# First load of an encoder kernel in single k tiles, with the first weight tile split by VectorE

## The reference

```
layer 0:  h = RMSNorm(x) @ w_in        # 2048 x 8192: q, k, v, gate
          per head (8): a = softmax(q1 k1 + bias) - lam * softmax(q2 k2 + bias);  o = a @ v
          x += (head_norm(o) * silu(gate)) @ w_out
layer 1:  h = RMSNorm(x) @ w_in + b    # 2048 x 6144: a, g, z
          u = depthwise_conv31(a * sigmoid(g)); u = silu(LayerNorm(u)) * silu(z)
          x += u @ w_out + b_out
out = RMSNorm(x)
```

## Time and profile before

| | |
|---|---|
| median of 3 runs | 869.5 us (869.18, 869.5, 871.02) |
| span of the profiled execution | 867.2 us (its own time is not listed apart from the three runs) |
| TensorE busy | 855.9 us, 99% |
| VectorE, ScalarE, POOL busy | 567.5, 446.9, 215.6 us |
| mean granted clock of TensorE | 0.998 |
| HBM read | 160.83 MB |

### The profile page before, as it was taken

One profiled execution on the slowest core, in us unless ns is written; L12 is line 12 of the kernel. 1 busy time (PEld: TensorE's weight loads), 2 busy tenths in 40 slices (PEclk: granted clock), 3 DMA queues, 4 the chain that ended last, 5 costly groups with the idle time before them and its releaser, 6 DMA issues.

```text
span 867.2 us, 13867 instructions
## 1 busy us (share of the span) xinstructions
PE 855.9 (99%) x5732; PEld 782.8 (90%) x5732; DVE 567.5 (65%) x896; ACT 446.9 (52%) x582; POOL 215.6 (25%) x74
## 2 busy tenths in 40 slices
PE   8999999999999999999999999999999999999996
PEld 8998899889998899888888899999999999998885
DVE  6556564584456554585454557999999998566651
ACT  6745443455345543567444454455554555694432
POOL 0000000000000000000000006888888888680000
PEclk9999999999999999999999999999999999999999
DMA  9976565544554565543555654555555556549502
GB/s 338 395 259 234 164 195 193 184 162 157 196 193 145 163 199 190 194 146 116 179 191 194 194 175 164 194 172 175 193 195 171 174 191 196 167 173 340 177 19 97
DMA packets 97856, 163.74 MB, mean 189 GB/s; under 512 B 3296, under 2 KB 38368, under 8 KB 97288
## 3 DMA queue, kind: packets, MB, share of 16 engines
q1 hardware_dynamic: 96320, 160.77, 55.1%
q10 hardware_dynamic: 1480, 2.19, 0.7%
HBM read 160.83 MB, written 3.69 MB: 190 GB/s over the span
## 4 chain that ended last, share of the span: by engine, by line
PE 93%; DMA 3%; DVE 2%; ACT 1%; SPq 0%; issue 0%; ACTq 0%
PE ps_acc L1174 16%; PE ps_acc L1177 16%; PE ps_acc L1176 16%; PE ps_acc L1157 13%; PE ps_acc L1160 13%; PE ps_acc L1159 13%; DMA sb_xs<-in_x 2%; DMA sb_xT<-in_x_turned 1%; PE ps_a L1120 1%; PE ps_d L1120 1%; DVE sb_w_lo L766 1%; PE ps_a L1241 0%; PE ps_a L1240 0%; PE ps_a L1239 0%; PE ps_d L1218 0%; PE ps_d L1217 0%
## 5 line engine op out<-in xcount | busy, mean ns | idle before, releaser
L417 ACT ACTIVATE sb_w_hi<-sb_w_raw 128x2048 fp32r<-128x2048 f32 x141 | 270.1, 1916 | 288.3 <-PE ps_acc L1177 186.4
L766 DVE TENSOR_TENSOR sb_w_lo<-sb_w_raw,sb_w_hi 128x2048 fp32r<-128x2048 f32 x97 | 222.3, 2292 | 170.1 <-ACT sb_w_hi L417 169.9
L1174 PE MATMUL ps_acc<-sb_conv_hi,sb_w_hi 128*128 128x256 f32 x768 | 215.5, 281 | 0.0
L1177 PE MATMUL ps_acc<-sb_conv_hi,sb_w_lo 128*128 128x256 f32 x768 | 214.3, 279 | 0.0
L1176 PE MATMUL ps_acc<-sb_conv_lo,sb_w_hi 128*128 128x256 f32 x768 | 214.2, 279 | 0.0
L408 POOL TENSOR_TENSOR sb_w_lo<-sb_w_raw,sb_w_hi 128x2048 fp32r<-128x2048 f32 x44 | 203.8, 4639 | 41.3 <-ACT sb_w_hi L417 41.3
L961 DVE SCALAR_TENSOR_TENSOR ps_d<-sb_uT,sb_dwT,ps_d 128x256 f32<-128x256 f32 x480 | 188.9, 481 | 4.5 <-ACT ps_d L648 4.5
L1157 PE MATMUL ps_acc<-sb_w_hi,sb_act_hi 128*128 128x512 f32 x384 | 152.4, 397 | 0.0
L1160 PE MATMUL ps_acc<-sb_w_hi,sb_act_lo 128*128 128x512 f32 x384 | 151.5, 394 | 0.0
L1159 PE MATMUL ps_acc<-sb_w_lo,sb_act_hi 128*128 128x512 f32 x384 | 151.5, 394 | 0.0
L1174 PE MATMUL ps_acc<-sb_act_hi,sb_w_hi 128*128 128x256 f32 x512 | 143.7, 281 | 2.0 <-DVE sb_w_lo L802 2.0
(11 more groups left out here) (167 smaller groups left out, 818.2 us busy)
## 6 DMA issues: line engine op xcount, KB each, us to landing
sb_w_raw<-in_attn_w_in SPq DMA_DIRECT2D x61, 1024.0 KB, 5.5
sb_w_raw<-in_conv_w_in SPq DMA_DIRECT2D x64, 512.0 KB, 4.5
sb_w_raw<-in_attn_w_out SPq DMA_DIRECT2D x16, 1024.0 KB, 4.9
sb_w_raw<-in_conv_w_in SPq DMA_DIRECT2D x16, 1024.0 KB, 5.0
sb_w_raw<-in_conv_w_out SPq DMA_DIRECT2D x16, 1024.0 KB, 5.0
sb_w_raw<-in_attn_w_in SPq DMA_DIRECT2D x6, 512.0 KB, 8.1
sb_xT<-in_x_turned SPq DMA_DIRECT2D x4, 512.0 KB, 8.1
sb_xs<-in_x SPq DMA_DIRECT2D x2, 1024.0 KB, 15.7
```

Source lines behind the costliest of these rows:

```text
L417: act.activation(w_hi[slot][:], w_raw[slot][:], ACT.Copy).then_inc(hi_ready, 1)
L766: dve.tensor_tensor(w_lo[slot][:], w_raw[slot][:], w_hi[slot][:].bitcast(F32), ALU.subtract).then_inc(lo_ready, 1)
L1174: pe.matmul(into, left_hi, hi[:, kt], start=(kt == 0 and f % 2 == 0), stop=False, skip_group_check=True)
L1177: ins = pe.matmul(into, left_lo, hi[:, kt], start=False, stop=(kt == KT - 1), skip_group_check=True)
```

## The change

The head is loaded and split in ten pieces (`HEAD`): k tiles 0, 1, 2, 3 singly, and six pairs. SyncE issues per piece the tiles of `xT` and of the weights; the weights of piece 0 are issued by ScalarE behind `vec_all`. VectorE makes the high part of piece 0's weights (`first_hi`), ScalarE that of the others. TensorE runs a single k tile kind by kind: four matmuls high times high, four with `act_lo`, four with `w_lo`, with a wait ahead of each kind; a pair waits once and runs as before. POOL writes `ones` ahead of everything else, TensorE starts on it alone, and runs 9 warm-up matmuls. The warm-up no longer waits for `ident`, nor for `d_free`.

```diff
-HALVED = 3
-WARM_UP = 12
+HEAD = [(k, k + 1) for k in range(CK)] + [(k, k + 2) for k in range(CK, KT, 2)]
+WARM_UP = 9
...
+        def head_piece(p):
+
+            k0, k1 = HEAD[p]
+            return k0 // CK, slice(k0 % CK, (k1 - 1) % CK + 1), k1 % CK == 0
+
+        def pieces_left_open(p):
+
+            return sum(k1 % CK != 0 for _, k1 in HEAD[:p])
+
+        def piece_landed(p):
+
+            slot, _, closes = head_piece(p)
+            return landed[slot] if closes else head_landed[pieces_left_open(p)]
...
-            for q in range(PAIRS):
-                sp.dma_start(xT[:, q * CK:(q + 1) * CK], x_turned[:, q * CK:(q + 1) * CK]).then_inc(x_landed[q], 16)
-                if q < HALVED:
-                    half = q * CK + CK // 2
-                    sp.dma_start(w_raw[q][:, 0:CK // 2], w_in[:, q * CK:half, 0:GW]).then_inc(head_landed[q], 16)
-                    sp.dma_start(w_raw[q][:, CK // 2:], w_in[:, half:(q + 1) * CK, 0:GW]).then_inc(landed[q], 16)
-                else:
-                    load(q, w_in[:, q * CK:(q + 1) * CK, 0:GW])
+            for p, (k0, k1) in enumerate(HEAD):
+                slot, rows, _ = head_piece(p)
+                sp.dma_start(xT[:, k0:k1], x_turned[:, k0:k1]).then_inc(x_landed[p], 16)
+                if p:
+                    sp.dma_start(w_raw[slot][:, rows], w_in[:, k0:k1, 0:GW]).then_inc(piece_landed(p), 16)
             sp.dma_start(table[:], rel_bias).then_inc(table_landed, 16)
...
+            pool.memset(ones[:], 1.0).then_inc(consts_ready, 1)
             pool.memset(grants[:, 0:1], 0.0).then_inc(w_free, RING)
             pool.memset(grants[:, 1:2], 0.0).then_inc(acc_free, 4)
...
             pool.memset(ident[:], 0.0).then_inc(consts_ready, 1)
-            pool.memset(ones[:], 1.0).then_inc(consts_ready, 1)
...
             act.dma_start(vec_all[:], vectors).then_inc(vecs_landed, 16)
-            act.wait_ge(consts_ready, 3)
-
-            act.activation(table_probe, ident[:, 0:1], ACT.Copy)
+            act.dma_start(w_raw[0][:, 0:1], w_in[:, 0:1, 0:GW]).then_inc(piece_landed(0), 16)
+            act.wait_ge(consts_ready, 1)
+
+            act.activation(table_probe, ones[:, 0:1], ACT.Copy)
             act.wait_ge(vecs_landed, 16)
 
-            for q in range(PAIRS):
-                act.wait_ge(x_landed[q], 16)
-                for kt in range(q * CK, (q + 1) * CK):
+            for p, (k0, k1) in enumerate(HEAD):
+                slot, rows, closes = head_piece(p)
+                act.wait_ge(x_landed[p], 16)
+                for kt in range(k0, k1):
                     act.activation(act_hi[:, kt], xT[:, kt], ACT.Copy, scale=vecs[:, G_IN, kt:kt + 1]
                                    ).then_inc(split_hi, 1)
-                if q < HALVED:
-                    act.wait_ge(head_landed[q], 16)
-                    act.wait_ge(w_free, RING)
-                    act.activation(w_hi[q][:, 0:CK // 2], w_raw[q][:, 0:CK // 2], ACT.Copy).then_inc(head_hi, 1)
-                    act.wait_ge(landed[q], 16)
-                    act.activation(w_hi[q][:, CK // 2:], w_raw[q][:, CK // 2:], ACT.Copy).then_inc(hi_ready, 1)
-                else:
-                    high_part(q, q, 1)
+                if p:
+                    act.wait_ge(piece_landed(p), 16)
+                    act.activation(w_hi[slot][:, rows], w_raw[slot][:, rows], ACT.Copy
+                                   ).then_inc(hi_ready if closes else head_hi, 1)
             for i in range(NCH - ST):
...
-            for q in range(PAIRS):
-                dve.wait_ge(x_landed[q], 16)
-                for kt in range(q * CK, (q + 1) * CK):
+            for p, (k0, k1) in enumerate(HEAD):
+                slot, rows, closes = head_piece(p)
+                if p == 0:
+                    dve.wait_ge(piece_landed(0), 16)
+                    dve.tensor_copy(w_hi[slot][:, rows], w_raw[slot][:, rows]).then_inc(first_hi, 1)
+                dve.wait_ge(x_landed[p], 16)
+                for kt in range(k0, k1):
                     dve.wait_ge(split_hi, kt + 1)
                     dve.scalar_tensor_tensor(act_lo[:, kt], xT[:, kt], vecs[:, G_IN, kt:kt + 1],
                                              act_hi[:, kt].bitcast(F32), ALU.mult, ALU.subtract
                                              ).then_inc(x_split, 1)
-                if q < HALVED:
-                    dve.wait_ge(head_hi, q + 1)
-                    dve.tensor_tensor(w_lo[q][:, 0:CK // 2], w_raw[q][:, 0:CK // 2],
-                                      w_hi[q][:, 0:CK // 2].bitcast(F32), ALU.subtract).then_inc(head_lo, 1)
-                    dve.wait_ge(hi_ready, q + 1)
-                    dve.tensor_tensor(w_lo[q][:, CK // 2:], w_raw[q][:, CK // 2:],
-                                      w_hi[q][:, CK // 2:].bitcast(F32), ALU.subtract).then_inc(lo_ready, 1)
+                if p == 0:
+                    dve.wait_ge(first_hi, 1)
+                elif closes:
+                    dve.wait_ge(hi_ready, slot + 1)
                 else:
-                    low_part(q, q)
+                    dve.wait_ge(head_hi, pieces_left_open(p))
+                dve.tensor_tensor(w_lo[slot][:, rows], w_raw[slot][:, rows], w_hi[slot][:, rows].bitcast(F32),
+                                  ALU.subtract).then_inc(lo_ready if closes else head_lo, 1)
             for i in range(NCH - 1):
                 low_part(RING + i, i)
...
-            pe.wait_ge(consts_ready, 3)
...
+            def head_slot(i):
+
+                for p, (k0, k1) in enumerate(HEAD):
+                    slot, rows, closes = head_piece(p)
+                    if slot != i:
+                        continue
+                    if k1 - k0 > 1:
+                        pe.wait_ge(x_split, k1)
+                        pe.wait_ge(lo_ready if closes else head_lo, i + 1 if closes else pieces_left_open(p + 1))
+                        for kt in range(k0, k1):
+                            ins = project_tile(i, 0, act_hi, act_lo, kt)
+                        continue
+                    kt = k0
+                    into = [acc[:, f // 2, (f % 2) * SEQ:(f % 2 + 1) * SEQ] for f in range(GW // P)]
+                    left = [[part[i][:, kt % CK, f * P:(f + 1) * P] for f in range(GW // P)] for part in (w_hi, w_lo)]
+                    pe.wait_ge(split_hi, kt + 1)
+                    if p == 0:
+                        pe.wait_ge(first_hi, 1)
+                    elif closes:
+                        pe.wait_ge(hi_ready, i + 1)
+                    else:
+                        pe.wait_ge(head_hi, pieces_left_open(p))
+                    for f in range(GW // P):
+                        pe.matmul(into[f], left[0][f], act_hi[:, kt], start=(kt == 0 and f % 2 == 0), stop=False,
+                                  skip_group_check=True)
+                    pe.wait_ge(x_split, kt + 1)
+                    for f in range(GW // P):
+                        pe.matmul(into[f], left[0][f], act_lo[:, kt], start=False, stop=False, skip_group_check=True)
+                    pe.wait_ge(lo_ready if closes else head_lo, i + 1 if closes else pieces_left_open(p + 1))
+                    for f in range(GW // P):
+                        ins = pe.matmul(into[f], left[1][f], act_hi[:, kt], start=False, stop=False,
+                                        skip_group_check=True)
+                ins.then_inc(w_free, 1)
 
             def pair_slot(j, i):
                 t, A = i // NCH, A_START + A_PER_PAIR * j
-                head = type(j) is int and j == 0 and i < HALVED
-                if head:
-                    pe.wait_ge(head_lo, i + 1)
-                    pe.wait_ge(x_split, CK * i + CK // 2)
+                if i % NCH == 0:
+                    pe.wait_ge(acc_free, 2 * (4 * j + t + 1))
+                if type(j) is int and j == 0 and i < NCH:
+                    head_slot(i)
                 else:
                     pe.wait_ge(lo_ready, 16 * j + i + 1)
-                if i % NCH == 0:
-                    pe.wait_ge(acc_free, 2 * (4 * j + t + 1))
-                halfway = (lambda: second_half(i)) if head else None
-                if t < 2:
-                    project_turned(i % NCH, t % 2, act_hi, act_lo, halfway)
-                else:
-                    project(i % NCH, t % 2, act_hi, act_lo, halfway)
+                    if t < 2:
+                        project_turned(i % NCH, t % 2, act_hi, act_lo)
+                    else:
+                        project(i % NCH, t % 2, act_hi, act_lo)
...
-            pe.wait_ge(d_free, 2)
+            pe.wait_ge(consts_ready, 1)
             for _ in range(WARM_UP):
                 pe.matmul(bank_d[0][:, 0:P], ones[:], ones[:], start=True, stop=True)
             for i in range(16):
-                if HALVED <= i < PAIRS:
-                    pe.wait_ge(x_split, CK * (i + 1))
                 pair_slot(0, i)
                 if i == 2:
...
```

(27 more changed lines are left out.)

12 lines of the change are left out of this document (6 added, 6 removed).

## The result

The changed kernel takes **871.78 us** (median of 13 runs, 869.59 to 873.51) where the kernel before took 869.54 on the same chip (13 runs, 868.82 to 871.02). The ratio is 1.0025, with a 95% interval of 1.0017 to 1.0033: slower by 2.2 us, a quarter of a per cent. The forecast was no change at 869.5.

The account below looks back on a forecast made before the run. TensorE, busy 99%, was taken as the bound, the spread's start set by the DMA stream. Head -2.6, spread's wait +2.6, stream 0 (-0.8 to +0.7): span 867.2, median 869.5 us; range 867.6 to 872.2.

Parts of the forecast that it names:

- The head's whole gain is then idle time in front of L1185: At the spread behind slot 4: TensorE's wait grows from 0.76 to 3.4 us, so the head gains nothing.
- The head, term by term: Warm-up, first weights and x, k tiles up to slot 4: TensorE some 2.6 us ahead, 3.6 with early `vec_all`.
- the other end of 4.3: Landing of `vec_all` in the head: taken as 5.3 us, at the earliest 4.3.
- rival B: At the spread: TensorE's clock falls in the new wait, price 2.7 us, time 872.2; chance 0.13, slower.
- The 2.0 us at 7.33 did no such harm: Old head's wait for the first low part: matmuls behind it came at the high clock level's pace.
- It may strike some executions only: Clock's fall in the wait at the spread: may hit only some executions, then the median stays; hence chance 0.13.
- the 2.3 us between span and median: Whole kernel: profiled span 867.2 against median 869.5 us, the difference taken as constant.
- The price: Low clock behind the wait at the spread: 5.5 us at half speed costs 2.7 us.
- The stream term: DMA loads ahead of the second row tile of `xs`: change of 0 us, between -0.8 and +0.7.
- the upper bound: DMA stream: `xT` in smaller pieces at the conv stage's 331 instead of 372 GB/s costs 0.7 us.
- The row that I called nearest: DMA stream: the head's own 2 KB weight pieces, 397 GB/s from 5 to 10 us, so zero cost.
- Rival C: Head's DMA loads: small loads slow the stream, row tile and spread 2 us late, 871.5; chance 0.05, slower.

Follow-up runs that it names:

- experiment 4: The changed kernel with the spread of the normalization factors moved one slot later, behind slot 5 in place of slot 4: 867.10 us, ratio 0.9974.
- Experiments 5 to 8: Kernel before: spread moved behind slot 5, 870.62 us; unedited, 870.58; moved spread traced again, 869.53; moved spread with 18 warm-up matmuls in place of 12, 867.97.
- experiment 6: The kernel before with no edit, taken once more for a second trace: 870.58 us, span 868.8.
- experiment 3: The changed kernel with 24 warm-up matmuls in place of 9: 871.45 us, ratio 1.0018.
- experiment 1: The changed kernel with 12 matmuls on `ones` ahead of the spread, behind slot 4: 870.10 us, ratio 1.0006.
- experiments 1 and 2: The changed kernel with matmuls on `ones` ahead of the spread: 12 of them, 870.10 us; 4 of them, 870.07 us.
- experiments 1 to 3: The changed kernel with 12 matmuls on `ones` ahead of the spread, 870.10 us; with 4, 870.07; with 24 warm-up matmuls and none there, 871.45.
- experiment 11: The changed kernel with the spread behind slot 5 and eight k tiles loaded and multiplied singly in place of four: 864.73 us, ratio 0.9942.
- experiment 9: The changed kernel with 12 matmuls on `ones` ahead of the spread and the last 12 k tiles of `xT` in three loads: 870.47 us, ratio 1.0010.

## Why the prediction was wrong

**The path was read rightly.** "The head's whole gain is then idle time in front of L1185" held: TensorE's wait there went from 0.76 to 3.66 us (3.4 forecast). The spread went on following the second row tile at the same distance of 4.7 us, and experiment 4 shows what happens once the spread stands elsewhere.

**The head, term by term.** The warm-up ran from 1.00 to 5.14, as forecast. `vec_all` landed at 3.96, earlier than even the other end of 4.3; what ended the wait for the first kind was VectorE's copy, which had itself waited until 4.87 for the first weights to land. The copy took 0.43 us, between the bounds of 0.3 and 0.6, and the low part of a single k tile 0.69, not 0.61:

```profile
4.87 0.43 DVE L806 CAST sb_w_hi<-sb_w_raw 128x512 fp32r<-128x512 f32 x1 [0.75 <-DMA sb_w_raw<-in_attn_w_in]
5.21 0.48 DVE L810 SCALAR_TENSOR_TENSOR sb_act_lo<-sb_xT,sb_vec_all,sb_act_hi 128x256 fp32r<-128x256 f32 x1
5.61 0.69 DVE L819 TENSOR_TENSOR sb_w_lo<-sb_w_raw,sb_w_hi 128x512 fp32r<-128x512 f32 x1
```

The first kind began at 5.45 (6.1 forecast). That gain was lost again at k tile 4, which started at 12.98 and not at 12.3. I had reckoned VectorE's time and not the landing: ScalarE waited 0.79 us for those weights and copied them only at 10.51, and VectorE 1.30 for ScalarE. So TensorE was 2.0 us ahead at the end of slot 4, not 2.6.

**The step that failed is rival B's chance.** It had the mechanism, the place and nearly the price. Against it I set "The 2.0 us at 7.33 did no such harm", and from "It may strike some executions only" I drew that the median would stay. Both rested on a single profiled execution, one of the minority that kept its clock. Experiments 5 to 8 show that the old wait of 2.0 to 3.2 us is followed by a low clock in three of the four traces that have the old head and its 12 warm-up matmuls, and in the timed executions of the kernel before at least 36 of 64 lost it (experiment 6). With the spread behind slot 5, six more warm-up matmuls are worth 2.65 us. The sum held a sign of this: I took the 2.3 us between span and median as constant, where the timed executions have 1.75 to 1.88. With a longer wait the harm was to be expected in most executions, and so it was: of the 13 runs of the change one kept a mean clock of 0.999, with 869.59 us; the other twelve had 0.994 to 0.997, with 870.97 to 873.51. The Trainium skill (TensorE: Matmul & The Clock Gate, Part 1) says that the number of cold matmuls at a kernel's start varies from run to run, and the traces agree: the 12 warm-ups of the kernel before took 5.49 us in one execution and 4.29 in another. The stretch behind the spread varies too, which that passage doesn't speak of: low from 39.1 to 45.9 us behind a wait of 3.7 here, and from 41.5 to 44.9 behind one of 3.9 in experiment 3.

The price was set at 2.7 us. Measured: 2.4 in the profiled execution, 1.5 in experiment 3, and 1.7 between the medians of the change and experiment 1. The 2.7 took 5.5 us from the warm-up and half of them as lost; where the clock fell in the traces it was mostly low for less, and the pace of 0.21 against 0.12 loses 0.44, not half.

**The stream term was mis-sized.** I took zero, between -0.8 and +0.7. By the medians of experiments 1 and 2 it is +0.6 and +0.5 over the kernel before, but both sides of that comparison hold some lost clock. Like with like are the executions at a mean clock of 0.999: 868.74 to 868.93 in eight of the kernel before, 869.59 in the one of the change, 869.65 to 870.10 in eight of experiments 1 to 3. That is +0.8 to +1.0, and the 0.9 by which the second square came later between the two profiles agrees. The other traces narrow it less: the square starts at 35.13, 35.71, 35.76, 35.61 and 35.66 with the old head, median 35.66, though the clock had fallen ahead of it in three of these, and at 36.04, 35.64, 37.54, 36.08, 35.89 and 36.05 in the six with the new head and all its pairs, median 36.05. So between +0.4 and +1.0, near the upper bound or over it. The row that I called nearest, 397 GB/s from 5 to 10 us, was the wrong choice. After the change it reads:

```profile
5.00:10.00 5.00, 4.69 (x40) 4.58 (x40) 4.87 (x11) 3.54 (x7) 0.00 (x0) 1.00 0.98 339
```

That is 346 per full share, near the 331 of the conv stage that I had kept as the upper bound. The share is still 0.98: the engines show as busy, and fewer bytes move. Over 5 us this is 0.29 MB less, 0.75 us at 383 GB/s; against it, from 2 to 3 us 262 GB/s moved where it had been 176, which gives back 0.2. Why the small loads run slower stays open. Rule and row go the same way here: the Trainium skill (DMA: Bandwidth & Descriptors, section Bandwidth) wants loads batched to 1 MiB, and the head did slow down with smaller ones. But size alone doesn't order the runs, since experiment 11, with more single tiles still, moved 377 GB/s in the same stretch, and experiment 9, with larger loads of `xT`, 348. Rival C had this mechanism with 2 us; it is a quarter to a half of that.

**The sum as it should have stood:** head -2.0, wait at the spread +2.0, stream +0.6, clock +1.7 in the median by experiment 1 (870.10 against 869.54 and 871.78), or stream +0.8, clock +1.4 by the executions at 0.999: the change's median lies 2.2 us above its own such execution, and that of the kernel before 0.7 to 0.8 above its. Either way 869.5 + 2.2 = 871.7 against a measured 871.78. How the 2.2 divide stays open by that much: the interval of experiment 1 alone leaves the stream between -0.3 and +1.3 us, and the change has only one execution at 0.999.

## What to carry to other kernels

A gain on one engine is worth what the next join lets through: before shortening the head, look for the first instruction behind it that waits for something else, and move it or its input. TensorE's idle time can cost more than its length, here from waits of 2.0 us on and not in each execution, so a wait that is merely moved and gathered in one place can make a kernel slower; idle matmuls were worth 1.7 us in the wait and 2.65 ahead of it. What the latter are worth in the kernel before with the spread in its old place was not run; its executions at 0.999 lie 0.7 us under its median. A single profiled execution doesn't show that a gap is harmless: compare the mean clock and the time of all runs with its own, and look twice.
